# Thirty-two of 256 tokens fetch their experts' rows, and the other 224 go through the dense expert products

## The reference

```python
def peer_ffn(xn, w_query, sub_keys, expert_u, expert_v):
    ...
    s_top, i_top = lax.top_k(s, PEER_TOPK)          # 16 of 128 keys, for each of 8 heads and 2 halves
    ...
    g_s, sel = lax.top_k(cand, PEER_TOPK)           # 16 of the 256 sums
    idx = jnp.take_along_axis(cand_idx, sel, axis=-1)
    g = jax.nn.softmax(g_s, axis=-1)
    ...
        u = jnp.take(expert_u, ic, axis=0)
        a = jnp.einsum('td,thkd->thk', xc, u).astype(jnp.float32)
        w = (gc * jax.nn.gelu(a, approximate=False)).astype(xc.dtype)
        v = jnp.take(expert_v, ic, axis=0)
        return jnp.einsum('thk,thkd->td', w, v)
```

## Time and profile before

| | us |
|---|---|
| median of 3 runs (lowest, highest) | 3020.96 (3019.37, 3028.45) |
| profiled execution: its span; no other time of its own is given | 3026.7 |
| block 1: U1, U2, V1, V2 | 184.3, 219.4, 173.3, 176.0 |
| block 2: U1, U2, V1, V2 | 184.4, 219.6, 173.0, 176.0 |

### The profile page before, as it was taken

The page is one execution under the profiler, slowest core; times in us unless marked ns, Lnnn a source line. Parts: engine busy times, 40 slices in busy tenths (PEclk is TensorE's granted clock), DMA queues, the critical chain, the costliest instruction groups (busy, mean ns, idle before and its releaser), DMA issues.

```text
span 3026.7 us, 49552 instructions
## 1 busy us (share of the span) xinstructions
PE 2927.1 (97%) x19456; PEld 2652.4 (88%) x19456; DVE 2173.4 (72%) x3232; ACT 1353.5 (45%) x1497; POOL 560.4 (19%) x311
## 2 busy tenths in 40 slices
PE   5998899999999999999999999999999999999999
PEld 4888788888899888799999988788999999988887
DVE  7788678888875755669867755566769967755565
ACT  4444454454534544544444444444344444444443
POOL 2310313123030210018810000000008830000000
PEclk9999999999999999999999999999999999999999
DMA  7776147877733655145566756676445556755685
GB/s 295 282 275 240 70 164 278 286 257 268 272 137 112 237 170 179 56 168 182 182 207 230 242 193 222 238 279 218 171 178 181 182 202 235 241 196 208 248 287 201
DMA packets 147054, 640.73 MB, mean 212 GB/s; under 512 B 12456, under 2 KB 46416, under 8 KB 90464
## 3 DMA queue, kind: packets, MB, share of 16 engines
q1 hardware_dynamic: 127104, 568.02, 53.3%
q10 hardware_dynamic: 19808, 70.79, 6.3%
HBM read 604.14 MB, written 34.62 MB: 211 GB/s over the span
## 4 chain that ended last, share of the span: by engine, by line
PE 63%; DVE 2%; DMA 2%; ACT 1%; issue 1%; DVEq 0%; ACTq 0%
PE pp L1280 8%; PE pp L1281 8%; PE pp L1282 8%; PE mz L1347 7%; PE mz L1349 7%; PE mz L1350 7%; PE pp L577 5%; PE pp L579 2%; PE pp L588 2%; PE pp L590 2%; PE pp L589 2%; PE mz L1323 2%; DMA raw<-expert_v 1%; DVE w_lo L1954 1%; ACT w_hi L1408 1%
## 5 line engine op out<-in xcount | busy, mean ns | idle before, releaser
L1954 DVE TENSOR_TENSOR w_lo<-raw,w_hi 128x2048 fp32r<-128x2048 f32 (+1 forms) x416 | 911.5, 2191 | 434.1 <-ACT w_hi L1408 433.3
L1408 ACT ACTIVATE w_hi<-raw 128x2048 fp32r<-128x2048 f32 (+1 forms) x486 | 893.8, 1840 | 566.5 <-DMA raw<-expert_v 366.3
L1280 PE MATMUL pp<-hs,w_hi 128*128 128x256 f32 x2048 | 585.8, 286 | 0.0
L1281 PE MATMUL pp<-hs,w_hi 128*128 128x256 f32 x2048 | 580.3, 283 | 0.0
L1282 PE MATMUL pp<-hs,w_lo 128*128 128x256 f32 x2048 | 580.2, 283 | 0.0
L577 PE MATMUL pp<-hs,w_hi 128*128 128x512 f32 x1408 | 512.0, 407 | 24.4 <-POOL hs L2840 12.9
L2783 POOL TENSOR_TENSOR w_lo<-raw,w_hi 128x2048 fp32r<-128x2048 f32 x64 | 319.6, 5007 | 1021.1 <-ACT w_hi L1408 1021.1
L1347 PE MATMUL mz<-w_hi,w_split 128*128 128x512 f32 x1024 | 402.7, 393 | 8.8 <-DVE w_split L2612 8.6
L1349 PE MATMUL mz<-w_lo,w_split 128*128 128x512 f32 x1024 | 400.8, 391 | 0.0
L1350 PE MATMUL mz<-w_hi,w_split 128*128 128x512 f32 x1024 | 400.6, 391 | 0.0
L579 PE MATMUL pp<-hs,w_lo 128*128 128x256 f32 x1408 | 399.8, 284 | 0.0
(11 more groups left out here) (328 smaller groups left out, 4148.3 us busy)
## 6 DMA issues: line engine op xcount, KB each, us to landing
raw<-expert_u SPq DMA_DIRECT2D x128, 1024.0 KB, 4.8
raw<-expert_v SPq DMA_DIRECT2D x128, 1024.0 KB, 4.8
raw<-ffn_in SPq DMA_DIRECT2D x88, 1024.0 KB, 4.9
ada_raw<-ada ACTq DMA_DIRECT2D x116, 512.0 KB, 5.3
raw<-ffn_down SPq DMA_DIRECT2D x64, 704.0 KB, 5.0
raw<-out_w SPq DMA_DIRECT2D x16, 1024.0 KB, 4.8
raw<-hgrn SPq DMA_DIRECT2D x16, 1024.0 KB, 4.8
raw<-query SPq DMA_DIRECT2D x16, 1024.0 KB, 4.8
```

The costliest lines, as they stand in the source:

```text
L1280: mm(dst, wh, hs[:, k, 0, :], start=(k == 0), stop=False, skip_group_check=True)
L1281: mm(dst, wh, hs[:, k, 1, :], start=False, stop=False, skip_group_check=True)
L1408: f(w_hi[:, slot, 0:n], raw[:, slot, 0:n], ACT.Copy).then_inc(hi_ready, 1)
L1954: v.tensor_tensor(w_lo[:, slot, 0:n], raw[:, slot, 0:n], w_hi[:, slot, 0:n].bitcast(F32), ALU.subtract)\
```

## The change

Tokens 0 to 31 (`FEW`) leave the dense products. For each of them the 128 experts' rows are fetched by index. Four copies of the 32 tokens fill the 128 partitions, so 32 fetches (`FEW_STEPS`) of 128 rows of 4 KB bring all rows of `expert_u`, and 32 more those of `expert_v`. GpSimd issues them as indirect transfers into rings of three tiles (`ROW_RING`). VectorE takes the dot of each row with its token (`few_dot`) and later adds the weighted rows up (`few_add`); eight small matmuls with a constant `fold` add the four copies into the dense sums. The dense products go over 224 tokens (`TD`). In the second ones the roles change: weights are stationary, the split activations move (448 columns for high and low together, 224 for the weights' low part), 32 matmuls a chunk, and the result comes out with features on partitions, so `y_tok` and its turns go. There are 28 steps of gates for 32, and they run three chunks late (`LEAD`). In U2 GpSimd makes `w_lo` of the odd chunks from the second pair on, VectorE that of the even ones. Some semaphores are shared between parts that before had their own.

The new and changed parts of the schedule, cut to those that the text speaks of:

```diff
+FEW = 32
+TD = T - FEW
+COPIES = P // FEW
+FEW_STEPS = HEADS * TOPK // COPIES
+ROW_RING = 3
+UNITS = TD // UNIT_T
+STEPS = TD // STEP_T
+LEAD = 3
...
+def few_dots_at(n):
+    at = lambda c: min(FEW_STEPS, ROW_RING + 2 * min(c, LEAD) + max(c - LEAD, 0))
+    return range(at(n), at(n + 1))
...
@@ PE: first products, gates, second products @@
-                                mm(dst, wh, hs[:, k, 0, :], start=(k == 0), stop=False, skip_group_check=True)
-                                mm(dst, wh, hs[:, k, 1, :], start=False, stop=False, skip_group_check=True)
-                                last = mm(dst, wl, hs[:, k, 0, :], start=False, stop=(k == KD - 1), skip_group_check=True)
+                                mm(dst, wh, hs[:, k, 0, FEW:T], start=(k == 0), stop=False, skip_group_check=True)
+                                mm(dst, wh, hs[:, k, 1, FEW:T], start=False, stop=False, skip_group_check=True)
+                                last = mm(dst, wl, hs[:, k, 0, FEW:T], start=False, stop=(k == KD - 1), skip_group_check=True)
...
-                            spread(n, j)
+                        if spread and not (isinstance(n, int) and not 0 <= n - LEAD < STEPS):
+                            spread(n - LEAD, 1 - j)
...
+                def down_tile(half, j, e, k, start):
+                    a = e * D + k * P
+                    acc = bank_of(k)
+                    mm(acc[:, 0:2 * TD], w_hi[:, 2 * half + j, a:a + P], w_split[:, j, e].rearrange("p a t -> p (a t)"),
+                       start=start, stop=False, skip_group_check=True)
+                    return mm(acc[:, 0:TD], w_lo[:, 2 * half + j, a:a + P], w_split[:, j, e, 0], start=False, stop=False,
+                              skip_group_check=True)
...
@@ ScalarE, U2, step n @@
                         split_next(ph, rp, pair, half, lap, j)
-                        if n:
-                            gate_copy(n - 1)
+                        if n > LEAD:
+                            gate_copy(n - LEAD - 1)
...
                         gelu(act_out[:, j], pair, half, j)
...
@@ VectorE, after the top 16 of a block @@
+                dve.wait_ge(few_cp, l + 1)
+                for i in range(ROW_RING):
+                    few_dot(i)
                 dve.wait_ge(best_e, l + 1)
...
@@ VectorE, U2 @@
+                for rp, pair, half, lap in each_pair(ph):
+                    for j in range(2):
+                        n = 2 * rp + j
+                        if 0 <= n - LEAD - 1 < STEPS:
+                            times(n - LEAD - 1, (n - LEAD - 1) % 2)
+                        if 0 <= n - LEAD + 1 < STEPS:
+                            build(n - LEAD + 1, (n - LEAD + 1) % 2)
+                        if rp == ph.pairs - 1:
+                            split_next(ph, rp, pair, half, j)
+                        elif j == 0:
+                            split_even(pair + 1, 1 - half)
+                        for i in few_dots_at(n):
+                            few_dot(i)
...
+                def few_dot(i):
+                    b = i % ROW_RING
+                    dve.wait_ge(row_in[b], row_count(l, 0, i))
+                    v.scalar_tensor_tensor(fetched_u[b][:], fetched_u[b][:], 1.0, x_rows[:], ALU.mult, ALU.mult,
+                                           accum_out=few_act[:, i:i + 1]).then_inc(dot_done, 1)
...
@@ VectorE, V1 @@
                                 split_next(ph, rp, pair, half, j)
+                                few_add(2 * rp + j)
...
@@ GpSimd @@
+                def fetch_u(i):
+                    if i == 0:
+                        pool.wait_ge(few_in, 16 * COPIES * (2 * l + 1))
+                    if i >= ROW_RING:
+                        pool.wait_ge(dot_done, FEW_STEPS * l + i - ROW_RING + 1)
+                    b = i % ROW_RING
+                    g_.indirect_dma_start(out=fetched_u[b][:], out_offset=None, in_=rows_u,
+                                          in_offset=bass.IndirectOffsetOnAxis(ap=few_idx[:, i:i + 1], axis=0)).then_inc(row_in[b], 16)
...
+                ph = plan[("expert_u", 2 * l)]
+                for rp, pair, half, lap in each_pair(ph):
+                    for j in range(2):
+                        split(pair + 1, 1 - half, j, lo_ready)
+                        n = 2 * rp + j
+                        if 22 <= n < 22 + ROW_RING:
+                            fetch_u(n - 22)
+                ph = plan[("expert_u", 2 * l + 1)]
+                for rp, pair, half, lap in each_pair(ph):
+                    if rp < ph.pairs - 1:
+                        split(pair + 1, 1 - half, 1, lo_pool)
+                    for j in range(2):
+                        for i in few_dots_at(2 * rp + j):
+                            fetch_u(i)
+                for i in range(FEW_STEPS):
+                    fetch_v(i)
```

More of the change, by code:

```diff
@@ L193, in build @@
 def build(nc, x, cols, const, pick, lvmask, rel, bucket, c_row, ada, ffn_in, ffn_down, attn, out_w, hgrn, swa, conv,
-          query, keys, expert_u, expert_v, out):
+          query, keys, expert_u, expert_v, rows_u, rows_v, out):
     plan, PAIRS = stream_plan()
@@ L1271, in up @@
                         n = 2 * rp + j
-                        pe.wait_ge(lo_ready, 2 * pair + j + 1)
+                        if spread and j and not (isinstance(rp, int) and rp == 0):
+                            pe.wait_ge(lo_pool, (HALF_CHUNKS // 2 - 1) * (q // 2) + rp)
+                        else:
+                            pe.wait_ge(lo_ready, 2 * pair + j + 1)
                         if not fresh:
@@ L1340, in peer @@
                             for e in range(2):
[L1341 to L1346, removed]
-                                        mm(acc, w_split[:, j, 0, e, tok], wh, start=(first and e == 0), stop=False,
-                                           skip_group_check=True)
-                                        mm(acc, w_split[:, j, 0, e, tok], wl, start=False, stop=False, skip_group_check=True)
-                                        last = mm(acc, w_split[:, j, 1, e, tok], wh, start=False, stop=False,
-                                                  skip_group_check=True)
@@ L1352, in peer @@
[L1352 to L1363 removed]
+                                for k in range(KD):
+                                    last = down_tile(half, j, e, k, False)
@@ new lines, in down_last @@
+                def down_last(ph, q):
+                    pair, half = ph.pair0, ph.pair0 % 2
+                    down_waits(q, ph.rp0, pair, 0)
+                    for e in range(2):
+                        for k in range(KD):
+                            last = down_tile(half, 0, e, k, False)
+                    last.then_inc(w_used, 1)
+                    down_waits(q, ph.rp0, pair, 1)
+                    for k in range(KD):
+                        for e in range(2):
+                            last = down_tile(half, 1, e, k, False)
+                        if k % 2 and k < KD - 1:
+                            last.then_inc(y_mm, 1)
+                    last.then_inc(w_used, 1)
@@ L1365, in _ @@
+                ph = plan[("expert_v", 2 * l)]
+                assert plan[("expert_u", 2 * l + 1)].pair0 % 2 == 1
+                down_first(ph, 2 * l)
+                down(ph.part(1, ph.pairs - 1), 2 * l)
+                ph = plan[("expert_v", 2 * l + 1)]
+                down(ph.part(0, 2), 2 * l + 1)
+                few_fold(l)
+                down(ph.part(2, ph.pairs - 3), 2 * l + 1)
+                down_last(ph.part(ph.pairs - 1, 1), 2 * l + 1)
             pe.wait_ge(ones_in, 16)
@@ L1955, in split_one, with split_even @@
                  .then_inc(lo_ready, 1)
+            def split_even(pair, half):
+                dve.wait_ge(hi_ready, 2 * pair + 1)
+                v.tensor_tensor(w_lo[:, 2 * half], raw[:, 2 * half], w_hi[:, 2 * half].bitcast(F32), ALU.subtract).then_inc(lo_ready, 2)
             def split_next(ph, rp, pair, half, j):
@@ L2847, in _ @@
             for l in range(2):
-                split_phase(plan[("expert_u", 2 * l)])
+                experts(l)
 def buckets(dist):
```

297 lines of the change are left out of this document (187 added, 110 removed).

## The result

The changed kernel takes 3234.16 us (median of 4 runs, 3222.12 to 3234.69), the kernel before 3024.7 on the same chip (4 runs, 3019.37 to 3034.96): a ratio of 1.068, interval 1.066 to 1.071. It is slower by 206 us on the profiled spans (3232.7 against 3026.7), where 144 were forecast.

A forecast was written before the change was run, and what follows sets the result against it. TensorE (PE) was taken to set the pace everywhere before the change. Per block +1 +83 +0 -8 -4 = +72, twice +144, gives 3171 on the profiled 3026.7, so 3165 for the median; own range 3110 to 3235, chance 0.73.

The forecast's parts named there:

- U2: Stage with the second half of the expert_u products, gates spread between chunks: 299 us against 215.6, +83 a block.
- Products: Dense matmuls on PE: 224-column first products 0.110 us each, second-product pairs 0.310; 15.4 us a stage for PE alone.
- U1: First products of experts 0 to 63: gates ready at 1529, gain gone, +1 us a block (bounds -12 and +11).
- V1: First expert_v stage: bound by the weight slot, 5.4 us a chunk, no gain, 0; +11 if landing takes 6.
- F: Fetch of rows in U2, issue to landing: taken as 5.5 us, between 3.7 and 8.5, counted 13 times.
- PE's stall: In U2, PE stands still for about 9 us in each pair of chunks, until step 25.
- the ring: In U2, four in-order queues wait on each other in a loop: 20.9 us a pair, 13.5 now.
- the weight slot: In V1, chain from chunk n-2's end through landing, splits, add and next chunk: 16.1 us for three chunks, 0.4 of it hand-overs.
- V2: Second expert_v stage: same chain with weigh for few_add, 5.2 us a chunk against 5.5; -8 (bounds -15 and 0).
- Seams: Outside the stages: y_tok copies and turns go, few_fold is new, V1 starts shorter; -4 a block.
- The fetch is dearer: Rival, chance 0.12: with F at 8.5 us, 2 x 39 us more, 3243, or 3265 with a crowded V1.
- five with two inputs: In U1, five VectorE instructions ahead of the gates may each stand behind a GpSimd subtract (4.6 us).

The follow-up runs named there:

- E3: The changed kernel without fetches, dots, adds and fold, so tokens 0 to 31 get nothing from the experts: 2965.23 us, ratio 0.982.
- E1: The changed kernel, but in U2 GpSimd issues a pair's fetches ahead of its subtract, not behind it: 3079.87 us, ratio 1.021.
- E5: E2 without the fetches of expert_v rows; adds stay at full width on a tile already there: 2997.78 us, ratio 0.993.
- E6: E2 with all fetches, but adds from the second row on cover 64 of 1024 columns: 3010.05 us, ratio 0.996.
- E2: The changed kernel, but in U2 VectorE makes all of w_lo and GpSimd only fetches: 3030.66 us, ratio 1.004.
- E4: The changed kernel, but in V1 VectorE does few_add ahead of w_lo, not behind it: 3220.4 us, ratio 1.067.
- E7: E2 with expert_v fetches and adds spread over V1 and V2, adds ahead of w_lo, fold at the end of V2: 3002.25 us, ratio 0.993.
- E8: E7 with the first three dots in U1 behind the gates, not ahead of them: 2999.32 us, ratio 0.994.

## Why the prediction was right, and where it was short

**Products.** Right. First products over 224 columns start 0.11 us apart, a product pair of the second kind 0.31 us after the one before (forecast 0.110 and 0.310). The starts of PE in U1 and V1:

```profile
1450.00 0.27 PE L1327 MATMUL pp<-hs,w_hi 128*128 128x224 f32 x1
1450.11 0.27 PE L1328 MATMUL pp<-hs,w_lo 128*128 128x224 f32 x1
...
1999.77 0.38 PE L1399 MATMUL mz<-w_split,w_hi 128*128 128x448 f32 x1
1999.98 0.27 PE L1401 MATMUL mz<-w_split,w_lo 128*128 128x224 f32 x1
2000.08 0.38 PE L1399 MATMUL mz<-w_split,w_hi 128*128 128x448 f32 x1
```

**U1.** Right: +0.9 and +0.7 for +1. PE is done early and waits 11.8 and 11.5 us for `gate_n`; it goes on at 1530.5, forecast 1529. The number has luck in it, for it was the middle of a wide span (1516 to 1539), and not all hold-ups fell where it said: the three dots took 1.22 us each and `h_few` 1.23, free of any subtract, and the two index operations 2.2 and 4.5, while `gate_n`, which it counted at its own time, took 3.99 us for 0.42 beside one. E3, without the dots, has U1 at 177 and 172.

**U2.** Right in mechanism and in size, a round of 20.4 us for 20.9 and F of 5.3 for 5.5, +85 and +86 for +83. E1 turned one link and took 71 us a block away. Only PE's stall was off, 6 us for 9, which the ring doesn't feel.

**V1.** This is the step that failed: "What binds is the weight slot: from the end of chunk n-2, landing 4.8, ... No gain. If the added 512 KB a chunk bring the landing to 6, +11. I take 0." The slot does bind, but the landing was taken from a trace without the indirect fetches; it is 5.7 us in the median and up to 7. The case with the crowded landing was the right one, and its price was low as well: +15 and +25, not +11. Two terms of the chain were too small. The sum of links was 15.7 us for three chunks; with a landing of 5.7 it is 16.6, and with the 1.2 us of hand-overs that V2 shows below, for my 0.4, it is 17.8. Times 32/3 that is 190 us, and block 1 has 190.8. This was put together after the result. The same sum without the fetches gives 180, and E5 has 177; with adds of 0.28 us for 1.28 it gives 179, and E6 has 182 and 184. So it puts the add too high, 11 us where E6 measures 7, and the fetches too low, 10 where E5 measures 13. Why block 2 loses 10 us more than block 1 in the change, at a clock of 0.95 and a landing of 5.9, and not in E2 (190.6 and 189.7), wasn't found; V1 of block 2 is 191 in E1 and 176 in E4, whose V1 should be like that of the change but for the add.

**V2.** -3.5 twice for -8. E3 shows that the 32 tokens aren't the reason. In this stretch ScalarE waits for the weights to land and VectorE for ScalarE:

```profile
ACT w_hi L1508 <- DMA raw<-expert_v: 89.0, 29, 4.4
DVE w_lo L2067 <- ACT w_hi L1508: 64.1, 31, 3.4
```

so the slot chain binds as forecast, but at 5.5 us a chunk (176.3/32), not 5.2. Three chunks are 16.5 us, and the durations of the links (landing 4.9, `w_hi` 1.9, `w_lo` 2.3, `weigh` and `low` 0.6 each, the chunk's products 5.0) sum to 15.3: 1.2 us are hand-overs, where I had 0.4. This is worked out from rows; no run tests it.

**Seams.** Nothing for -8. The end is 3 us shorter (from the last second product to the span's end 4.0 us for 7.2), as forecast, and the stretches ahead of each block took that back (1.3 and 2.3 us).

**The rivals.** "The fetch is dearer" has the time (3243 to 3265) nearer to the measured 3234 than the forecast, for a wrong reason: F didn't grow. That the forecast's own range held the time is in part luck: it reached 3235, the time is 3234, and V1 used more than its bound while F used nothing of its own. The profiled execution lies 1.5 us under the median here, where that of before lay 6 above: this offset is 7 of the 69 us by which the forecast is short.

## What to carry to other kernels

An issue of a transfer is an instruction in an in-order queue: write down what stands ahead of it, and put it ahead of long work, not behind it (71 us a block here for two swapped items). Where a stage is bound by the way of a slot, from its load to its next load, the landing time of before is no constant: transfers that the change adds in that stage make it longer (4.8 to 5.7 us here). And price the dense part first: E3's 1.8% was the whole purse, and with the 32 tokens' rows well placed (E7, E8) 0.7% of the span was left.

## What was not expected of the hardware

GpSimd's subtract holds up more of VectorE than instructions with two SBUF inputs. In U1 of the change, VectorE instructions with a single tile as input took these times, the first of them beside this subtract:

```profile
1495.78 4.64 POOL L2939 TENSOR_TENSOR w_lo<-raw,w_hi 128x2048 fp32r<-128x2048 f32 x1
...
1495.87 9.26 DVE L2649 CAST top_b<-top_i 128x256 bf16<-128x256 uint32 x1
...
1505.19 4.62 DVE L2651 TENSOR_SCALAR sel_u<-best_i 128x128 uint32<-128x128 uint32 x1
```

In block 1 of the kernel before they took 0.50 and 0.22 us, the first at the very end of a subtract and the second beside none. The next subtracts start at 1500.35 and 1505.10, so the cast stood still through two of them, one right behind the other. The Trainium skill (SBUF — State Buffer, SBUF: two separate sides) counts VectorE operations in a two-port mode among those that exclude a GpSimd operation, as well as those with two SBUF inputs. The durations agree with that, though in which mode these two ran no trace shows, and my count of "five with two inputs" was too narrow a rule. It did not hurt the sum, as the gates' time was taken from the middle of its bounds.
